# The area of y is placed 352 bytes past a multiple of 1024

## The reference

```
h = rms_norm(x, norm_g[layer]) * (1.0 + scale[:, None, :]) + shift[:, None, :]
y = even_mixer(h, ...)  or  odd_mixer(h, ...)      # (y * silu(g)) @ w_out
x = x + gate[:, None, :] * y
```

## Time and profile before

| | |
|---|---|
| median of 3 runs | 1300.48 us (1300.39 to 1300.86) |
| the profiled execution | 1300.32 us, span from its first to its last instruction 1298.5 us |
| mean granted tensor clock | 0.999 of full |
| HBM | 220.3 MB read, 170 GB/s over the span |

### The profile page before, as it was taken

How to read it: one execution, slowest core, us unless ns; L and a number is a source line. 1 busy time by engine, 2 the same in 40 slices (tenths; PEclk the granted TensorE clock), 3 DMA queues, 4 the chain that set the end, 5 groups by cost and what they waited for, 6 DMA issues and landing times.

```text
span 1298.5 us, 24906 instructions
## 1 busy us (share of the span) xinstructions
PE 1270.7 (98%) x10560; PEld 1148.1 (88%) x10560; DVE 815.8 (63%) x1245; ACT 694.8 (54%) x901; POOL 92.2 (7%) x73
## 2 busy tenths in 40 slices
PE   6999999999999999999999999999999999999997
PEld 5998899889999999999888888999999899888886
DVE  4667766876656867666655545556868657655533
ACT  2556546865766566245544435766566335544432
POOL 0000000000001320230000000000330140000000
PEclk9999999999999999999999999999999999999999
DMA  9866756624434433225555554434433225555452
GB/s 386 301 237 264 278 201 235 228 98 161 137 136 157 159 130 131 68 98 179 178 194 176 182 194 162 163 130 163 157 136 106 91 69 180 192 194 184 174 177 82
DMA packets 35102, 222.93 MB, mean 172 GB/s; under 512 B 3888, under 2 KB 8240, under 8 KB 9264
## 3 DMA queue, kind: packets, MB, share of 16 engines
q1 hardware_dynamic: 31248, 216.23, 47.0%
q10 hardware_dynamic: 3744, 5.11, 1.2%
HBM read 220.28 MB, written 1.05 MB: 170 GB/s over the span
## 4 chain that ended last, share of the span: by engine, by line
PE 89%; DVE 5%; ACT 2%; DMA 2%; issue 1%; SPq 0%; ACTq 0%; DVEq 0%
PE pj L630 60%; PE yv L630 14%; PE sc L630 9%; PE tp L630 4%; DVE ring_rounded L744 2%; PE tp L496 1%; DMA ring<-weights 1%; PE tp L1885 1%; DMA xT<-x_t 1%; DVE att_area L573 1%; ACT w_split L735 0%; DVE big L1848 0%; ACT att_area L527 0%; DVE yT_rounded L1840 0%; DVE scr L1692 0%
## 5 line engine op out<-in xcount | busy, mean ns | idle before, releaser
L744 DVE TENSOR_TENSOR ring_rounded<-ring,w_split 128x2048 fp32r<-128x2048 f32 x108 | 253.2, 2347 | 49.6 <-ACT w_split L735 47.2
L735 ACT CAST w_split<-ring 128x2048 fp32r<-128x2048 f32 x106 | 201.9, 1904 | 35.5 <-PE pj L630 26.4
L2111 DVE TENSOR_TENSOR ring_rounded<-ring,big_rounded 128x2048 fp32r<-128x2048 f32 x66 | 151.3, 2292 | 107.3 <-ACT big_rounded L1982 107.2
L630 PE MATMUL pj<-h_split,w_split 128*128 128x256 f32 x1264 | 174.5, 289 | 0.2 <-ACT w_split L2361 0.2
L630 PE MATMUL pj<-h_split,ring_rounded 128*128 128x256 f32 x1264 | 167.8, 283 | 1.1 <-DVE ring_rounded L744 1.1
L630 PEld LDWEIGHTS pj<-h_split,w_split 128*128 128x128 f32 x1264 | 157.8, 191 | 7.2 <-issue 5.1
L630 PEld LDWEIGHTS pj<-h_split,ring_rounded 128*128 128x128 f32 x1264 | 158.4, 192 | 2.6 <-DVE ring_rounded L744 1.8
L1982 ACT CAST big_rounded<-ring 128x2048 fp32r<-128x2048 f32 x66 | 126.2, 1912 | 49.9 <-PE pj L630 48.2
L630 PE MATMUL pj<-hT_rounded,w_split 128*128 128x256 f32 x1136 | 148.3, 283 | 0.0
L630 PEld LDWEIGHTS pj<-hT_rounded,w_split 128*128 128x128 f32 x1136 | 141.6, 192 | 0.0
L1352 POOL TENSOR_TENSOR big<-big 128x512 f32<-128x512 f32 x16 | 30.7, 1918 | 766.5 <-DVE big L1281 758.3
(11 more groups left out here) (366 smaller groups left out, 2160.4 us busy)
## 6 DMA issues: line engine op xcount, KB each, us to landing
ring<-weights SPq DMA_DIRECT2D x180, 1024.0 KB, 4.9
big<-weights SPq DMA_DIRECT2D x20, 1024.0 KB, 7.7
first_block<-biases ACTq DMA_DIRECT2D x26, 192.0 KB, 5.1
first_block<-biases SPq DMA_DIRECT2D x6, 192.0 KB, 11.4
xT<-x_t SPq DMA_DIRECT2D x1, 1024.0 KB, 9.3
out_t<-scr SPq DMA_DIRECT2D x4, 256.0 KB, 2.9
con<-constants SPq DMA_DIRECT2D x1, 897.0 KB, 6.7
aux<-small SPq DMA_DIRECT2D x1, 832.0 KB, 11.7
```

Of the source, the lines that this page charges most:

```text
L630: return nc.tensor.matmul(out, lhsT, rhs, start=start, stop=stop, skip_group_check=True)
L735: act.post(nc.scalar.copy(w_split[:, w % 2], ring[:, in_ring(idx)]), s["w_high"])
L744: dve.post(nc.vector.tensor_tensor(ring_r[:, at], ring[:, at], w_split[:, w % 2].bitcast(F32), ALU.subtract), s["w_low"])
L2111: dve.tell(nc.vector.tensor_tensor(w_low(t, i), w, value(w_high(i)), ALU.subtract), s["ffn_low"])
```

## The change

Four small buffers, `rt` (160 bytes a partition), `diag` (128), `cs` (32) and `fg2` (32), are declared straight behind the high part of h, and y behind them. 160 + 128 + 32 + 32 = 352, so y begins 352 bytes past a multiple of 1024. The areas before it in the new order keep their places or move by 8192 bytes. The smaller areas behind y shift by 192 bytes within 1024.

```diff
         big2, big2_r = with_rounded("big2", [P, 32 * SEQ])
-        yT, yT_r = with_rounded("yT", [P, KC, SEQ])
         scr, scr_r = with_rounded("scr", [P, KC, SEQ])
         rw, rw_r = with_rounded("rw", [P, 4, 8, P])
         first = nc.alloc_sbuf_tensor_at("first_block", [P, 6 * 384], F32, offset=nc.sbuf_base - 4 * 4 * 8 * P)
         bias = first[:, :].rearrange("p (b j) -> p b j", b=BIAS_RING)
         w_split = sb("w_split", [P, 2, SLOT], F32R)
         hh = sb("h_split", [P, KC, SEQ], F32R)
+        rt = sb("roots", [P, 40])
         diag = sb("diag", [P, 32])
+        cs = sb("cs", [P, 8])
+        fg2 = sb("final_squares", [P, KC])
+        yT, yT_r = with_rounded("yT", [P, KC, SEQ])
         mod_raw = sb("mod_raw", [P, 24])
-        cs = sb("cs", [P, 8])
         rstd = sb("rstd", [P, 2, SEQ])
...
         eps = sb("eps", [P, 4])
-        rt = sb("roots", [P, 40])
-        fg2 = sb("final_squares", [P, KC])
         kk_roots, hgrn_roots, rwkv_roots = (rt[:, a:a + 8] for a in (16, 24, 32))
```

## The result

The changed kernel takes 1305.32 us (1304.82 to 1305.54, six runs) where the kernel before takes 1300.65 (1300.39 to 1300.96, six runs). The ratio is 1.0035 with a 95% interval of 1.0023 to 1.0048: 4.7 us slower. The profiled execution took 1305.17 us with a span of 1303.4.

The account below looks back on a forecast made before the run. TensorE was taken as the bound, busy 98% of the span and 89% of the last chain. All four parts were priced at 0, so 1300.5 us was predicted, with a range of 1297 to 1313.5 us.

Parts of the forecast that it names:

- rival (a): One-pass operand reads in units wider than 352's alignment make y's matmuls slower: 12.1 us, 1312.6 us; chance of slower 0.28.
- Part 1: Feed-forward stage, 704 matmuls of 512 columns with y stationary: no change taken, near bounds +9.2 and -8.6 us.
- d: Change in step time of each of 704 feed-forward matmuls with y stationary; taken as 0.
- near bound: Upper bound for feed-forward steps with y stationary: the fixed 13.1 ns doubles, +9.2 us over 704 matmuls.
- fixed part: The 13.1 ns of a one-pass matmul step beyond 106.9 ns per 256 columns; the prediction's unit of price.
- Part 2: Output projections, 224 matmuls of 256 columns streaming y's low part: 0 taken, bounds +2.9 and -2.7 us.
- Parts 3 and 4: VectorE and ScalarE on moved areas, and plain float32 matmuls on areas behind y: cost 0 each.
- Rival (b): Next weight load collides with the streaming operand within 1024 bytes; y escapes, 12.2 ns a step, 11.3 us faster; chance 0.12.
- the page's step: The skill page's 256-column matmul step, N columns plus about 2.5 ns, 109 ns, against 120.0 in the trace.
- One for one: Feed-forward stage: PE has no slack, so any step change reaches the end in full, as long as it gets longer.

Follow-up runs that it names:

- w_128_y_256: Against the kernel before, high part of the weights moved 128 bytes and y 256 bytes past a multiple of 1024; 1297.69 us, ratio 0.9977.
- y_off_64: Against the kernel before, y placed behind the high part of h, 64 bytes past a multiple of 1024; 1304.56 us, ratio 1.0029.
- all_off_32: Against the kernel before, a 32-byte buffer added in front of the ring, moving every area alike; 1300.68 us, ratio 1.0001.
- h_before_64: Against the kernel before, high part of h declared in front of everything, all other areas 64 bytes later within 1024; 1290.32 us, ratio 0.9921.
- w_off_64: Against the kernel before, only the high part of the weights moved, 64 bytes past a multiple of 1024; 1292.62 us, ratio 0.9939.
- h_off_64: Against the kernel before, only the high part of h moved, 64 bytes past a multiple of 1024; 1296.07 us, ratio 0.9964.

## Why the prediction was right or wrong

**The time.** 1305.3 us lies in the range and not near the forecast of 1300.5. That the range held it is owed to rival (a), a mechanism that the runs rule out, and so it is luck. The forecast itself, no change with 0.60, was wrong, and so was its main step.

**Part 1, y as stationary operand, is the step that failed.** It set d = 0; d was 6.7 ns on 704 matmuls with what falls on their neighbours, 4.7 us, half of the near bound of 13.1. The neighbours with the low part of h, which the prediction held to be unchanged, took 0.9 us of it. Its reasons had a gap each. The slices at 0 and 512 past a multiple take the same step; w_128_y_256 shows the same for 256, so 0 and 512 are not two different cases. The transposes of raw are plain float32, and they are indeed unmoved after; the text said they don't bear on the fixed part of the rounded form, and then took them as the nearest rows all the same. Both rows were read correctly and say nothing on the question. A row that keeps the same relation as every other row can't price a change of that relation.

**Part 2, y as streaming operand,** came out as said: 0 (1.92 us for 16). It was right by luck. At 32 or 64 bytes the same products were 2 ns a step faster, and after this change their starts are 116 to 125 ns apart in turn, where they were an even 120; only the mean stayed at 120.

**Parts 3 and 4** held: the rows on raw stayed within 1 ns in the median, and VectorE and ScalarE are busy for 815.8 and 694.8 us before and after.

**Rival (a)** had the direction and half the size, and the wrong mechanism. It reasoned from the address of one operand. y_off_64 excludes a unit of 64 bytes, all_off_32 the operand's own address altogether.

**Rival (b)** had the mechanism nearly right, two operands of the same product that get in each other's way by their distance, and the wrong sign for this case: with 512 columns distance 0 is the best of those tried, and the change left it. With 256 columns its sign is right: 2.2 or 6.7 ns a step vanish at a distance of 64. Its bound of 12.2 ns is nearly twice the larger of the two. The argument against it in the prediction (slices 512 apart pay the same) fails for the same reason as in part 1.

By the Trainium skill (TensorE: Matmul & The Clock Gate, Step-by-step: what each phase is for) the weight load and the streaming operand have read ports of their own and don't take bandwidth from each other. The runs don't show where the two operands meet, but they show that the step depends on how the two lie to each other: the same products take 120.0 ns at distance 0 and 113.3 or 117.8 at 64. Independent ports are thus no reason to price a change of the distance at nothing. The prediction saw the 11 ns between the page's step and the trace's and didn't ask why. The 16-byte lines of the Trainium skill (SBUF — State Buffer, Door 1: The DMA port swizzle) don't explain it either: 32, 64, 128 and 352 are all multiples of 16 and all cost with 512 columns.

**Sums.** "One for one" was right in the feed-forward stage for a loss: 4.70 us from the stage's ends, 4.67 between the medians. For gains in the mixers it isn't: 13.8 us of shorter steps gave 10.1 in h_before_64, and 11.8 gave 8.2 in w_off_64.

**What stays open.** That the distance and not the address makes the difference is shown; what collides is not. Nor is the distance all: at 64 bytes runs of the same product have one of two steps, and the steps with the low part of h got longer beside those of the moved y. The runs can't tell whether the next weight load meets the stream, or the two reads share something else. Nor do they say why 512 columns prefer a distance of 0 and 256 columns one of 64, or what a step would be at distances between those tried.

## What to carry to other kernels

Where PE is the bound and its steps are short, look at the fixed part of a step (the steps of two widths give it) and treat the layout of SBUF as part of the kernel: a buffer added ahead of an operand can move the time by some tenths of a percent either way. Test it by moving one area by 32 or 64 bytes, and move everything by the same amount as a control. Before pricing a change at nothing, ask whether any row of the trace has the property that changes; if all rows share one value of it, they bound nothing.

## What the runs showed of the hardware

- The step of a matmul of rounded float32 operands depends on the distance of its two SBUF operands: 113.3 to 120.0 ns with 256 columns, 226.9 to 234 ns with 512, at the full granted clock.
- Distances of 0, 256 and 512 gave the same steps. The sign counts: with 512 columns +64 gives 233 to 234 ns and -64 gives 228 to 231.
- With 256 columns at +64 or -64 a run takes 113.3 or 117.8 ns a step throughout: 29 of 65 runs had the lower step at +64 in w_off_64, 8 of 142 at -64 in h_off_64.
- The address of an operand by itself didn't matter: 32 bytes added in front of everything left 1300.68 us.
- Plain float32 products, VectorE and ScalarE showed nothing of this: products of y in branch 1 215.9 ns a step before and after, transposes of raw 272 ns, its VectorE and ScalarE rows within 1 ns in the median.
